# RWKV output norm over four chunks at once, with the modulation rows and the merge's gate projections reordered

## The reference, cut to what matters

```python
yf = merge_dirs(y).astype(jnp.float32)           # 256 tokens, 8 heads of 64
mean = jnp.mean(yf, axis=-1, keepdims=True)
var = jnp.mean(jnp.square(yf - mean), axis=-1, keepdims=True)
y = ((yf - mean) * lax.rsqrt(var + LNX_EPS)).reshape(bsz, length, C_B) * lnx_g + lnx_b
bonus = jnp.einsum('blhn,bldhn,hn->blh', r_h, k_dir, r_k)[..., None] * v_h
y = (y + bonus.reshape(bsz, length, C_B)) * gate      # gate = sigmoid(g_lo) @ g2
...
g_a, g_b = jnp.split(gates, 2, axis=-1)               # gates: columns of u @ w_in
y = jax.nn.sigmoid(g_a) * (o_a @ w_o_a) + jax.nn.sigmoid(g_b) * (o_b @ w_o_b)
y = y @ w_out
...
h = h + m[2] * y
h = h + m[5] * hier_moe(modulate(rmsnorm(h, g), m[3], m[4]), ...)
```

## Time and profile before

| what | value |
|---|---|
| three timed runs | 3104.59, 3094.57, 3099.58 us; median 3099.58 us |
| profiled execution, its own time | 3092.36 us |
| its span from first to last instruction | 3090.6 us |
| mean granted TensorE clock | 0.902 of full speed |
| busy share: PE, DVE, ACT, POOL | 84%, 29%, 13%, 3% |
| mean DMA rate over the span | 255 GB/s |

### The profile page before, as it was taken

One profiled execution on the slowest core, in us unless ns is written; L12 is line 12 of the kernel. 1 busy time (PEld: TensorE's weight loads), 2 busy tenths in 40 slices (PEclk: granted clock), 3 DMA queues, 4 the chain that ended last, 5 costly groups with the idle time before them and its releaser, 6 DMA issues. The chain is left out here.

```text
span 3090.6 us, 43919 instructions
## 1 busy us (share of the span) xinstructions
PE 2585.5 (84%) x19739; PEld 1398.1 (45%) x19739; DVE 900.4 (29%) x1834; ACT 411.6 (13%) x811; POOL 85.4 (3%) x93
## 2 busy tenths in 40 slices
PE   7969568999999998889999899865666877869995
PEld 4525234334333343434433344343665876645553
DVE  0227543102212122221312031135448532143222
ACT  1032001100100001111211121011113221010001
POOL 0010000000000000000000000000000100000000
PEclk9988668899999999999999999986788988979998
DMA  5317037898999988988898979951010012159997
GB/s 183 109 41 268 33 127 291 339 390 333 388 380 371 364 359 354 403 345 342 336 396 354 371 295 368 378 189 61 1 35 1 3 57 99 68 224 419 422 422 293
DMA packets 158868, 789.17 MB, mean 255 GB/s; under 512 B 18241, under 2 KB 20553, under 8 KB 110937
## 3 DMA queue, kind: packets, MB, share of 16 engines
q1 hardware_dynamic: 155225, 773.78, 63.1%
q0 software_dynamic: 3456, 12.58, 1.0%
HBM read 774.79 MB, written 11.53 MB: 254 GB/s over the span
## 5 line engine op out<-in xcount | busy, mean ns | idle before, releaser
L2975 PE MATMUL bank<-ring,arena 128*34 128x512 f32 (+1 forms) x3072 | 700.0, 599 | 76.1 <-DMA ring<-in_w_up 61.9
L2975 PEld LDWEIGHTS bank<-ring,arena 128*34 128x34 f32 x3072 | 177.7, 117 | 490.5 <-issue 467.1
L2999 PE MATMUL bank<-ring,arena 128*34 128x512 f32 x1408 | 321.6, 600 | 46.2 <-DMA ring<-in_w_down 45.4
L2999 PEld LDWEIGHTS bank<-ring,arena 128*34 128x34 f32 x1408 | 80.0, 112 | 278.0 <-issue 152.3
L303 PE MATMUL bank<-arena,ring 128*128 128x256 f32 (+1 forms) x688 | 158.7, 394 | 11.8 <-DMA ring<-in_w_in 9.7
L303 PEld LDWEIGHTS bank<-arena,ring 128*128 128x128 f32 x688 | 134.0, 195 | 36.7 <-issue 10.5
L3439 PE MATMUL bank<-ring,arena 128*64 128x256 f32 x992 | 111.1, 379 | 3.2 <-DMA ring<-in_moe_w_up 2.4
L2875 PEld LDWEIGHTS bank<-arena 64*64 64x64 f32 x2304 | 76.8, 141 | 53.0 <-issue 52.6
L313 PE MATMUL bank<-ring,arena 128*128 128x512 f32 (+1 forms) x224 | 98.8, 596 | 0.0
L3439 PEld LDWEIGHTS bank<-ring,arena 128*64 128x64 f32 x992 | 72.7, 137 | 45.2 <-issue 12.5
L2987 PEld LDWEIGHTS bank<-consts,arena 34*128 34x128 f32 x704 | 82.4, 191 | 14.9 <-issue 14.1
(11 more groups left out here) (630 smaller groups left out, 3018.1 us busy)
## 6 DMA issues: line engine op xcount, KB each, us to landing
ring<-in_w_gate SPq DMA_DIRECT2D x128, 1408.0 KB, 9.2
ring<-in_w_up SPq DMA_DIRECT2D x128, 1408.0 KB, 12.3
ring<-in_w_down SPq DMA_DIRECT2D x176, 1024.0 KB, 8.5
ring<-in_w_in SPq DMA_DIRECT2D x46, 1024.0 KB, 6.7
ring<-in_moe_w_down SPq DMA_DIRECT2D x33, 1024.0 KB, 14.9
ring<-in_moe_w_gate SPq DMA_DIRECT2D x31, 1024.0 KB, 13.6
ring<-in_moe_w_up SPq DMA_DIRECT2D x31, 1024.0 KB, 16.5
ring<-in_ada_w SPq DMA_DIRECT2D x24, 1024.0 KB, 7.0
```

Of the source, the lines that this page charges most:

```text
L2975: last = mm(ps[c][row:row + CAP, 0:n], xsT[:, e, k, :], w[:, at:at + n], start=k == 0, stop=k == KT - 1)
L2999: last = mm(ps[6][row:row + CAP, :], hidT[:, 2 * j + f, :], w[:, f, half * BANK:(half + 1) * BANK], start=j + f == 0, stop=j == FT // 2 - ...
```

## The change

The norm works on all four chunks at once: sixteen groups of 64 values in each instruction. PE turns the normed values by 64x64 blocks, as plain matmuls against the identity, straight into banks 2 and 3, with no block-diagonal copy. DVE's gain and bias instructions read those banks. The bonus product is one instruction behind the request for the square root. The gate product goes to banks 4 and 5. `gains2` comes first on DVE, and the modulation rows first on PE, so the barrier between the norm and the rows is gone. Lastly the merge projects its four gate groups in a row, into banks 6/7, 0/1, 2/3 and 4/5, and then the four branch groups, each into the same banks, once its sigmoid is read out. `sgate` has four buffers, placed above the norm's tiles. The pieces are issued in the new order.

```diff
-        yb7 = ar(4 * C7, ...); mean7, var7 = ar(4), ar(4); yx7 = spread()
+        yb7 = ar(16 * C7, ...); mean7, var7 = ar(16), ar(16)
+        y_groups = yacc.rearrange("p c q v -> p (c q) v")
-        top[0] = rwkv_floor
-        sgate = [ar(4 * SEQ, "p (c t) -> p c t", c=4) for _ in range(2)]
+        sgate = [ar(4 * SEQ, "p (c t) -> p c t", c=4) for _ in range(4)]
-        merge_pieces = [column_pieces(... gates ...) + [piece(... w_o ...)] for g, br in MERGE]
+        merge_gate_pieces = [column_pieces(A["w_in_2"], A_COLS + B_COLS + br * D + g * 512, 512) for g, br in MERGE]
+        merge_out_pieces = [[piece(... w_o ...)] for g, br in MERGE]
+        MERGE_BANKS = (6, 0, 2, 4)
-        N_PHASES_M = N_PHASES_R2 + 2
+        N_PHASES_M = N_PHASES_R2 + 1
ACT
-            for c in range(NCL): wait sqrt_asked; Sqrt of var7
-            barrier
-            rows 0, 2, 4, 6
+            row_act(0, gain_row)
+            row_act(2, shift_row)
+            act.wait_ge(sqrt_asked, due(act, sqrt_asked))
+            ACTV(var7, var7, ACT.Sqrt, scale=1.0 / C7, bias=lnx_eps).then_inc(sqrt_ready, up(sqrt_ready))
+            row_act(4, m5_row)
+            row_act(6, mod_row)
             for n in range(4):
-                act.wait_ge(piece_used, after(merge_pieces[n][:2]))
-                if n >= 2: act.wait_ge(merge_read, due(act, merge_read))
+                act.wait_ge(piece_used, after(merge_gate_pieces[n]))
                 Sigmoid of two banks into sgate[n]
DVE
+            STT(gains2, ...).then_inc(gains2_ready, up(gains2_ready))
+            settled(nc.vector.tensor_reduce(mean7, y_groups, AX_X, ALU.add))
+            settled(TS(mean7, mean7, 1.0 / C7, None, ALU.mult))
+            settled(TT(y_groups, y_groups, in_groups(mean7), ALU.subtract))
+            settled(TT(yb7, y_groups, y_groups, ALU.mult))
+            nc.vector.tensor_reduce(var7, yb7, AX_X, ALU.add).then_inc(sqrt_asked, up(sqrt_asked))
+            TT(bonus, bonus, vT7, ALU.mult)
+            dve.wait_ge(sqrt_ready, due(dve, sqrt_ready))
+            settled(nc.vector.reciprocal(var7, var7))
+            TT(y_groups, y_groups, in_groups(var7), ALU.mult).then_inc(y7_ready, up(y7_ready))
+            dve.wait_ge(turned, due(dve, turned))
+            for q in range(4):
+                last = TS(yT7[:, q, :], ps[2 + q // 2][:, q % 2 * SEQ:(q % 2 + 1) * SEQ], pc("rwkv_lnx_g_2", q), pc("rwkv_lnx_b_2", q), ALU.mult, ALU.add)
+            last.then_inc(merge_read, up(merge_read))
+            settled(TT(yT7, yT7, bonus, ALU.add))
+            dve.wait_ge(gate7_ready, due(dve, gate7_ready))
+            four TT of yT7 by the gate in ps[4 + q // 2] into obT; the last adds to merge_read
PE
-            four chunks: transpose of yx7 by 128x128; gate product into banks 4 to 7; barrier
             row_of_columns_pe(0, gains2), (2, mod 3), (4, mod 5), (6, mod 2)
-            pe.wait_ge(m_row_read, due(pe, m_row_read, 4))
+            pe.wait_ge(m_row_read, due(pe, m_row_read, 3))
+            pe.wait_ge(g2_landed, due(pe, g2_landed, 16))
+            for q in range(4):
+                last = mm(ps[4 + q // 2][:, q % 2 * SEQ:(q % 2 + 1) * SEQ], g2sb[:, q * P:(q + 1) * P], gl, start=True, stop=True)
+            pe.wait_ge(y7_ready, due(pe, y7_ready))
+            for q in range(4):
+                for c in range(NCL):
+                    for h in range(2):
+                        last = mm(ps[2 + q // 2][r, at:at + C7], yacc[r, c, q, :], ident[r, r], start=True, stop=True)
+            pe.wait_ge(m_row_read, due(pe, m_row_read))
+            for n in range(4):
+                if n >= 2:
+                    pe.wait_ge(merge_read, due(pe, merge_read))
+                two_in_a_bank(pe, MERGE_BANKS[n], merge_gate_pieces[n], u2x_lat)
             for n, (g, br) in enumerate(MERGE):
+                pe.wait_ge(sgate_ready, due(pe, sgate_ready))
+                two_in_a_bank(pe, MERGE_BANKS[n], merge_out_pieces[n], (oaT, obT)[br])
-            pe.wait_ge(merge_read, due(pe, merge_read, 2))
+            pe.wait_ge(merge_read, due(pe, merge_read, 4))
```

More of the change, by code:

```diff
@@ L1360, in _, with row_act @@
             act.wait_ge(phase_ended, phase_end(act))
[L1361 to L1367, removed]
+            def row_act(base, row):
                 act.wait_ge(m_row_filled, due(act, m_row_filled))
@@ L1371, in _ @@
                 last.then_inc(m_row_read, up(m_row_read))
+            row_act(0, gain_row)
[4 more added lines that the diff above has]
+            row_act(6, mod_row)
             for n in range(4):
-                act.wait_ge(piece_used, after(merge_pieces[n][:2]))
-                if n >= 2:
-                    act.wait_ge(merge_read, due(act, merge_read))
+                act.wait_ge(piece_used, after(merge_gate_pieces[n]))
                 for b in range(2):
-                    last = ACTV(sgate[n % 2][:, 2 * b:2 * b + 2, :].rearrange("p c t -> p (c t)"), ps[4 * (n % 2) + b][:, :], ACT.Sigmoid)
+                    last = ACTV(sgate[n][:, 2 * b:2 * b + 2, :].rearrange("p c t -> p (c t)"), ps[MERGE_BANKS[n] + b][:, :], ACT.Sigmoid)
                 last.then_inc(sgate_ready, up(sgate_ready))
-                act.wait_ge(sgate_ready, own(act, sgate_ready))
             act.drain().then_inc(phase_ended, 1)
@@ L2268, in _ @@
             dve.wait_ge(phase_ended, phase_end(dve))
[L2270 to L2299, removed]
@@ new lines, in _ @@
+            STT(gains2, mods[:, 4 * KT:5 * KT, 0], 1.0, prm[:, PCOL["norm_ffn_g_2"]:PCOL["norm_ffn_g_2"] + KT], ALU.add, ALU.mult).then_inc(gains2_ready, up(gains2_ready))
+            in_groups = lambda v: v.unsqueeze(2).to_broadcast([P, 16, C7])
+            settled(nc.vector.tensor_reduce(mean7, y_groups, AX_X, ALU.add))
+            settled(TS(mean7, mean7, 1.0 / C7, None, ALU.mult))
+            settled(TT(y_groups, y_groups, in_groups(mean7), ALU.subtract))
+            settled(TT(yb7, y_groups, y_groups, ALU.mult))
@@ L2300, in _ @@
+            last.then_inc(merge_read, up(merge_read))
+            dve.wait_ge(merge_read, own(dve, merge_read))
+            settled(TT(yT7, yT7, bonus, ALU.add))
             dve.wait_ge(gate7_ready, due(dve, gate7_ready))
             for q in range(4):
-                TS(yT7[:, q, :], yT7[:, q, :], pc("rwkv_lnx_g_2", q), pc("rwkv_lnx_b_2", q), ALU.mult, ALU.add).then_inc(dve_order, up(dve_order))
-                dve.wait_ge(dve_order, own(dve, dve_order))
-                TT(bonus[:, q, :], bonus[:, q, :], vT7[:, q, :], ALU.mult).then_inc(dve_order, up(dve_order))
@@ L2306, in _ @@
[L2306 to L2315, removed]
+                last = TT(obT[:, q, :].rearrange("p (r w) -> p w r", r=ROWS7), yT7[:, q, :].rearrange("p (w r) -> p w r", r=ROWS7),
+                          ps[4 + q // 2][:, q % 2 * SEQ:(q % 2 + 1) * SEQ].rearrange("p (w r) -> p w r", r=ROWS7), ALU.mult)
@@ L2316, in _ @@
+            last.then_inc(merge_read, up(merge_read))
             for n, (g, br) in enumerate(MERGE):
-                dve.wait_ge(piece_used, after(merge_pieces[n][2:]))
+                dve.wait_ge(piece_used, after(merge_out_pieces[n]))
                 dve.wait_ge(sgate_ready, due(dve, sgate_ready))
@@ L2320, in _ @@
                 for b in range(2):
-                    last = TT(dst[:, 2 * b:2 * b + 2, :], sgate[n % 2][:, 2 * b:2 * b + 2, :],
-                              ps[4 * (n % 2) + 2 + b][:, :].rearrange("p (c t) -> p c t", c=2), ALU.mult)
+                    last = TT(dst[:, 2 * b:2 * b + 2, :], sgate[n][:, 2 * b:2 * b + 2, :],
+                              ps[MERGE_BANKS[n] + b][:, :].rearrange("p (c t) -> p c t", c=2), ALU.mult)
                 if br:
-                    last.then_inc(dve_order, up(dve_order))
-                    dve.wait_ge(dve_order, own(dve, dve_order))
+                    settled(last)
                     last = TT(merged[:, 4 * g:4 * g + 4, :], merged[:, 4 * g:4 * g + 4, :], term, ALU.add)
@@ L3348, in _ @@
             pe.wait_ge(phase_ended, phase_end(pe))
[L3349 to L3359, removed]
             def two_in_a_bank(pe, base, views, x):
@@ L3385, in _ @@
             row_of_columns_pe(6, mod_column(2))
[L3386 to L3389 removed]
+            pe.wait_ge(m_row_read, due(pe, m_row_read, 3))
+            pe.wait_ge(g2_landed, due(pe, g2_landed, 16))
+            for q in range(4):
+                last = mm(ps[4 + q // 2][:, q % 2 * SEQ:(q % 2 + 1) * SEQ], g2sb[:, q * P:(q + 1) * P], gl, start=True, stop=True)
+            last.then_inc(gate7_ready, up(gate7_ready))
+            pe.wait_ge(y7_ready, due(pe, y7_ready))
+            for q in range(4):
+                for c in range(NCL):
+                    at = q % 2 * SEQ + c * C7
+                    for h in range(2):
+                        r = half7(h)
+                        last = mm(ps[2 + q // 2][r, at:at + C7], yacc[r, c, q, :], ident[r, r], start=True, stop=True)
+            last.then_inc(turned, up(turned))
+            pe.wait_ge(m_row_read, due(pe, m_row_read))
```

(6 more changed lines are left out.)

12 lines of the change are left out of this document (4 added, 8 removed).

## The result

The changed kernel takes 3070.08 us (median of 4 runs, 3062.20 to 3075.27) against 3102.09 us before (4 runs). The ratio is 0.989, with a 95% interval from 0.9871 to 0.9908: faster by 32.0 us. Forecast were 33 us and 3066.6 us. The profiled execution took 3062.20 us, its span 3060.4 us.

What follows compares the result with a forecast made beforehand. Between scan and merge, PE and DVE alternate, each waiting for the other; afterwards PE bounds. Starting the merge 33.2 us earlier, taken as 33, gave 3099.58 - 33 = 3066.6 us; own range 3059 to 3073, chance 0.74.

Steps and rivals of the forecast that it cites:

- The merge's start: The merge's first matmul, the gate projection, was to start at 2550.1 instead of 2583.36, 33.2 us earlier.
- the stall before the gate product: PE, after the rows, was to wait 0.8 us for ACT's copy of the third row, until 2545.7.
- the turn: 32 matmuls of 64x64 against the identity, 64 records, on PE after the gate product: 2.7 us, ending at 2550.1.
- The reduction of 1024 numbers: In DVE's norm, absent from the earlier trace: between 1.22 and 1.68 us each, taken as 1.22.
- The clock at the front: After 1.9 us of idle PE behind the scan, a clock dip might cost 0 to 1.7 us; 0.3 taken.
- The dip before w_out: Half clock after 2.69 us of idle PE may fall away or stay: 0 to 1.7 us of gain, taken as 0.
- Rival B: The clock stays at 0.50 from 2539 until the gates; gain 20.4 us, 3079 us; chance 0.10.
- C: Rival: at the merge, PE waits for weights because transfers share engines or refills come late; gain 20 us, 3080 us; chance 0.06.
- D: Rival: the merge itself runs at 1.2 GHz, slower than before, wholly so ending at 3150 us; chance 0.03.
- The root: ACT's square root in the norm: table load and root 0.08 + 1.28 + 0.30 us, to 2544.5, without the skill's drain.
- The lower bound: Of the gain: 33.2 us less 1.7 (clock), 1.8 (slower reductions and passes) and 1 (turn), giving 29 us.
- the cover of DVE's gain, bonus and gate: These DVE instructions were to lie beneath the merge's first gate group (13.8 us); uncovered they would cost 5.6 us.

Runs made afterwards that it cites:

- the rows behind: Changed kernel, but PE makes the four modulation rows after the norm, the turn and DVE's gain, bonus and gate; 3079.13 us, ratio to before 0.9929.
- the merge in turn: Changed kernel, but gate group n and branch group n are projected one after the other, pieces issued in that order; 3065.72 us in one run.
- one row in the gap: Changed kernel, but the row of m[5] is made in PE's gap before w_out and ACT loads the root's table early; 3063.45 us, ratio to before 0.988.
- filler: Kernel with one row in the gap, plus sixteen unused 128x128 matmuls on PE in the router stage; 3064.51 us, ratio to before 0.9883; again 3064.14 us, 0.9866.
- the wide norm alone: Kernel before, with only the norm on all four chunks at once and the turn by 64x64 blocks; 3084.69 us, ratio to before 0.995.
- by chunks: Changed kernel, but the norm loops over four chunks of 128x256 with four roots, a row copy behind each of the first two; 3073.58 us in one run.
- by 128x128: Changed kernel, but DVE zeroes and fills a block-diagonal buffer and PE turns it by sixteen 128x128 transposes; 3060.75 us in one run.

## Why the prediction was right, by its own steps

- **The merge's start** was put 33.2 us earlier, and came 34.2 us earlier. PE's chain was 12.9 us from T in the forecast and 11.9 in the run. The rows took 7.38 (7.1 forecast), the stall before the gate product 0.19 (0.8), the product 1.9 to the next start (1.7), and the turn 2.0. **Two terms were mis-sized, the turn by 0.7 us and the stall by 0.6.** The turn's 2.7 us came from the earlier trace rows, a mean over 256 records of the scan, a part of which ran at 1.2 GHz; with the turn at that clock throughout, its 64 records take 3.58. The stall shrank as ACT's third copy ended 7.9 us behind T and not 8.4: the root came sooner (table load 5.3 us behind T, 5.7 forecast), and the copy took 0.98 us. The rows cost 0.3 us more than forecast, so that the errors partly cancel. The forecast's 1.78 us for a row is in no row either; the copies start 1.73 us apart.
- **The reduction of 1024 numbers** takes 1.21 to 1.22, the lower bound taken. DVE's product ends 8.5 us behind T (8.9 forecast), beneath PE's work.
- **The clock at the front** did not dip after 1.8 us of idle PE (0.3 us was set aside for it). The dip before w_out stayed. Rival B (a clock that stays low until the gates) is out: the windows show 1.00 throughout, and without the rows the clock does fall, to 0.50.
- **The merge** took 83.15 us for 384 records, as forecast, with no wait for a weight; C and D are out. Of the waits on `merge_read` none was felt.
- **The root** started 0.02 us behind the table load (2544.99 + 1.28, then 2546.29). The drain of 1.38 us that the Trainium skill (ScalarE: Activation LUTs, "What ACT_TABLE_LOAD costs") adds to a load isn't in this trace either.
- **The size of the step in the medians**: 33 forecast, 32.0 and 32.9 measured in two sets of runs.
- **The lower bound** took off 1.8 us for slower passes, though it says that 1.3 of it would be hidden. By its own terms 0.5 would reach the start, and the bound would be 30 us and not 29.

The prediction called the new order of the merge free and took it as the cover of DVE's gain, bonus and gate. The first holds; the cover was no merit of that order, since the old one covers them as well. Its price for them uncovered, 5.6 us, was 5.2 in the experiment with the rows behind. What the prediction did not say is how the gain divides. Of the 34.2 us, 16.4 hang on the two overlaps, the rows beside the norm and DVE's tail beneath the merge (3.9 of them the clock). 5.8 hang on the narrow norm in the place of the wide one, about 3 of them on ACT's order, and a further 2.2 would come in the merge. 1.2 hang on the turn by blocks, and none on the gates first. These don't add up to the whole: the removed barrier was not undone by itself, and the parts overlap.

## What to carry to other kernels

Where two engines hand small work back and forth, look for work of the idle engine that depends on neither and is needed anyway: here 7.4 us of it cost nothing and held the clock for what came next. Look past the start of a stage too: the narrow norm's waits cost another 2.2 us in the merge behind it, through the clock. And when a change has several parts, measure a fixed stretch of the profile, since the whole run may drift by more than a part is worth. Keep that stretch short, and compare its stages one by one: in S the clock's dips in stages that no edit touched were worth up to 4.1 us, more than several of the parts.

## What the runs showed of the hardware

- T moved between 2537.2 and 2554.9 us over twelve profiled executions of the same work up to T, while the stretch S of one kernel came out at 187.71 and 187.69. The timed runs of one kernel spread over 2.5 us (four runs) to 26.7 us (seven runs of before in one set). PE's waits for the first block's weights differ by a few microseconds between these runs (117 to 123 us), which is a part of it; the rest is open.
- The 32 MATMUL records of L3381 (its line in the changed kernel) in the router stage took 7.01 us at a clock of 0.50 in before, after (twice), and in the kernels with the merge in turn, with one row in the gap and with filler, and 4.5 to 5.0 us in the other five, beginning near 1.00. No edit touches them, and what decides is open.
- The same gap of 2.69 us before w_out was followed by a dip to half clock in before, after (twice), and in the kernels with the merge in turn, the rows behind and the wide norm alone (29.1 to 29.4 us), but not in those by chunks and by 128x128 (27.7). With a row in the gap there was none in four runs of three kernels. A gap of that size costs 1.5 us or nothing; which of the two it will be, the runs don't tell.
